# A decoder layer's feed-forward block on one NeuronCore: gate and up projections as seven half-size block products

## The reference

```python
def _ffn(x, w_gate, w_up, w_down, g, b):
    hdn = jax.nn.silu(x @ w_gate) * (x @ w_up)
    return _layer_norm(ALPHA * x + hdn @ w_down, g, b)
```

## Time and profile before

| what | value |
|---|---|
| median of three runs | 1817.17 us (1814.51 to 1818.33) |
| profiled execution, its span | 1820.0 us |
| TensorE busy | 1761.5 us (97%), 11328 matmuls |
| VectorE busy | 703.3 us (39%) |
| ScalarE busy | 371.5 us (20%) |
| GpSimd busy | 513.6 us (28%) |
| TensorE's mean granted clock | 0.975 of full speed |
| chain of work that ended last | TensorE 85%, VectorE 7% |

### The profile page before, as it was taken

One profiled execution on the slowest core, in us unless ns is written; L12 is line 12 of the kernel. 1 busy time (PEld: TensorE's weight loads), 2 busy tenths in 40 slices (PEclk: granted clock), 3 DMA queues, 4 the chain that ended last, 5 costly groups with the idle time before them and its releaser, 6 DMA issues.

```text
span 1820.0 us, 29093 instructions
## 1 busy us (share of the span) xinstructions
PE 1761.5 (97%) x11328; PEld 1615.3 (89%) x11328; DVE 703.3 (39%) x1255; ACT 371.5 (20%) x699; POOL 513.6 (28%) x296
## 2 busy tenths in 40 slices
PE   7999999998999999999999999999999999999995
PEld 6967677776877879999999899999999999999994
DVE  4156767541335261111174833313312312322327
ACT  4133232322233231111120640010010010010033
POOL 4210111110212023333353823333333333333325
PEclk9899999998998889999999999999999999999998
DMA  5144434304641122111112211111111111111102
GB/s 158 59 112 131 124 116 145 117 12 128 191 135 27 47 50 56 47 46 46 47 47 58 82 47 47 47 46 46 46 46 46 46 46 47 51 45 48 50 25 93
DMA packets 175297, 127.54 MB, mean 70 GB/s; under 512 B 22362, under 2 KB 148730, under 8 KB 175218
## 3 DMA queue, kind: packets, MB, share of 16 engines
q1 hardware_dynamic: 169586, 125.12, 23.3%
q10 hardware_dynamic: 5632, 1.35, 0.5%
HBM read 116.57 MB, written 9.87 MB: 69 GB/s over the span
## 4 chain that ended last, share of the span: by engine, by line
PE 85%; DVE 7%; DMA 2%; ACT 2%; issue 2%; SPq 2%; POOL 0%; DVEq 0%; ACTq 0%; POOLq 0%
PE psum L794 13%; PE psum L798 13%; PE psum L797 13%; PE psum L1355 4%; PE psum L1354 4%; PE psum L1350 4%; PE psum L855 4%; PE psum L859 4%; PE psum L861 4%; PE psum L1010 3%; PE psum L1303 2%; PE psum L1307 2%; PE psum L1306 2%; PE psum L983 2%; PE psum L939 1%
## 5 line engine op out<-in xcount | busy, mean ns | idle before, releaser
L733 POOL CAST wh<-raw 128x1024 fp32r<-128x1024 f32 x131 | 145.8, 1113 | 1258.9 <-PE psum L855 389.4
L794 PE MATMUL psum<-xh,wh 128*128 128x344 f32 (+1 forms) x1392 | 449.0, 323 | 3.6 <-POOL wl L735 3.4
L797 PE MATMUL psum<-xl,wh 128*128 128x344 f32 (+1 forms) x1392 | 446.2, 321 | 0.0
L798 PE MATMUL psum<-xh,wl 128*128 128x344 f32 (+1 forms) x1392 | 446.2, 321 | 0.0
L735 POOL TENSOR_TENSOR wl<-raw,wh 128x1024 fp32r<-128x1024 f32 x131 | 333.3, 2545 | 10.5
L794 PEld LDWEIGHTS psum<-xh,wh 128*128 128x128 f32 x1392 | 263.5, 189 | 5.3 <-issue 5.3
L797 PEld LDWEIGHTS psum<-xl,wh 128*128 128x128 f32 x1392 | 263.5, 189 | 0.5 <-issue 0.5
L798 PEld LDWEIGHTS psum<-xh,wl 128*128 128x128 f32 x1392 | 263.3, 189 | 0.0
L2457 DVE TENSOR_TENSOR hf<-sg,psum 128x344 f32<-128x344 f32 x66 | 33.8, 513 | 372.8 <-PE psum L798 363.7
L855 PE MATMUL psum<-xh,wh 128*128 128x352 f32 (+1 forms) x480 | 162.8, 339 | 1.5 <-DVE ql L1992 1.5
L859 PE MATMUL psum<-xl,wh 128*128 128x352 f32 (+1 forms) x480 | 161.1, 336 | 0.0
(11 more groups left out here) (332 smaller groups left out, 2702.7 us busy)
## 6 DMA issues: line engine op xcount, KB each, us to landing
raw<-in_w_in SPq DMA_DIRECT2D x86, 256.0 KB, 3.3
parts<-in_cache_k SPq DMA_DIRECT2D x64, 256.0 KB, 3.0
parts<-in_cache_v SPq DMA_DIRECT2D x64, 256.0 KB, 2.9
raw<-in_w_gate SPq DMA_DIRECT2D x44, 256.0 KB, 3.1
raw<-in_w_up SPq DMA_DIRECT2D x44, 256.0 KB, 3.1
raw<-in_w_down SPq DMA_DIRECT2D x44, 256.0 KB, 2.7
raw<-in_w_o SPq DMA_DIRECT2D x28, 256.0 KB, 3.1
cb<-negc_scratch SPq DMA_DIRECT2D x8, 520.0 KB, 5.4
```

What stands on the lines that cost most here:

```text
L733: pool.tensor_copy(wh[:, s, :], raw[:, r, :]).then_inc(sem("panel_high"), 1)
L794: first = mm(out, w[0], x[0], start=(n == 0), stop=False)
L797: mm(out, w[0], x[1], start=False, stop=False)
L798: last = mm(out, w[1], x[0], start=False, stop=(n == len(ks) - 1))
```

## The change

For groups 1 to 10 the product of a weight block by the activations, 256 by 1024 by 1032 for gate and again for up, is cut in two along each of the three sizes. The plain product of 2 x 2 blocks takes eight block products; the change makes it from seven with sums of blocks (Winograd's form of Strassen's method). With half sizes: hidden 128, model width 512 (four blocks of 128), tokens 516 (TH), which TensorE takes as two chunks of 258 columns (CW). One product is 2 x 4 x 3 = 24 matmuls.

- **Weights.** SP loads quarters of 128 by 512, 256 KB each (`quarter`), into six halves of `raw`. GpSimd makes the sums S1 = c + d, S3 = a - c, S2 = S1 - a, S4 = b - S2, and splits seven units of 512 columns for gate, seven for up and four for down, 18 a group, into six places of `wh` and `wl`; a place is free when TensorE has ended the unit six before (`room`, by `unit_done`).
- **Activations.** Three differences of blocks of x1 and a fourth that replaces a quarter of `xh` and `xl` are made once, in group 0, by VectorE (`t_make`, `t_low`) and ScalarE (`t_high`).
- **Products and combinations.** TensorE makes A11, S1, S3, S2, each in its own pair of banks, then A12, A22 and S4, which add onto the banks of A11, S3 and S1. ScalarE copies A11 and S1 out before that (`snaps`). VectorE makes the other blocks from these by adds (`combine`, and one add of two SBUF blocks, `c22`), ScalarE applies SiLU to gate's four blocks, and for up VectorE multiplies and splits the four hidden blocks.
- **Down** has its three chunks of 344 as before, from the new places (`down_new`); at its first chunk it waits for three of the four hidden blocks, and in its last chunk it tells GpSimd twice that weights are free, by waiting for its own last matmul.
- **Group 10** turns `mixed` within up's last three products, and makes the nine y tiles one after the other behind them.
- The loops over groups 1 to 9 on all engines are written out. Some buffers move.

The diff, cut to its core:

```diff
+UNITS_A_GROUP = 18
+A11, S1, S3, S2, A12, A22, S4 = range(7)
+BANKS_OF = {A11: 0, A12: 0, S1: 2, S4: 2, S3: 4, A22: 4, S2: 6}
+DOWN_BANKS = [6, 7, 0, 1, 4, 5, 2, 3]
...
+            def room(g):
+                if g >= 6:
+                    pool.wait_ge(sem("unit_done"), g - 5)
+                else:
+                    pool.wait_ge(sem("panel_used"), PAN_FFN + 4 + g // 2)
+            def unit_from(g, source):
+                high, lower = unit_of(wh, g), unit_of(wl, g)
+                step(pool.tensor_copy(high, source))
+                pool.tensor_tensor(lower, source, f(high), ALU.subtract).then_inc(sem("panel_split"), 1)
...
+                    come(n, ha, 0)
+                    room(g + A11)
+                    unit_from(g + A11, a)
+                    come(n, hc, 0)
+                    come(n, hd, job_)
+                    room(g + S1)
+                    s1 = unit_of(wlf, g + S1)
+                    step(pool.tensor_tensor(s1, c_, d, ALU.add))
+                    step(pool.tensor_tensor(c_, a, c_, ALU.subtract))
+                    step(pool.tensor_tensor(a, s1, a, ALU.subtract))
+                    unit_from(g + S1, s1)
...
-            with pe.Fori(0, FGROUPS - 2) as g:
-                B.loop(g, FFN_PER)
-                p = PAN_FFN + 6 + 6 * g
-                job(p, 0, A3, ALL8, X8, chunks=BODY)
-                job(p + 1, 1, B3, ALL8, X8, chunks=BODY)
-                job(p + 2, 2, A3, ALL8, X8, chunks=BODY)
-                job(p + 3, 0, B3, ALL8, X8, chunks=BODY)
-                down(g + 1, p)
-                B.end(FGROUPS - 2)
...
+            def product(n, job_, v, after=None):
+                g = unit_no(n, job_, v)
+                pe.wait_ge(sem("panel_split"), PANELS + g + 1)
+                b, begins = BANKS_OF[v], v in (A11, S1, S3, S2)
+                for c in range(2):
+                    out = psum[:, b + c, 0:CW]
+                    for k in range(4):
+                        x = moving(v, k, c)
+                        cols = slice(k * P, k * P + P)
+                        first = mm(out, wH[:, cols], x[0], start=(begins and k == 0), stop=False,
+                                   skip_group_check=True)
...
+                        mm(out, wH[:, cols], x[1], start=False, stop=False, skip_group_check=True)
+                        last = mm(out, wL[:, cols], x[0], start=False, stop=(k == 3), skip_group_check=True)
+                    if c == 0 and after is not None:
+                        after()
+                last.then_inc(sem("unit_done"), 1)
...
+            def seven(n, job_, turns=None):
+                for v in (A11, S1, S3, S2):
...
+                    product(n, job_, v)
+                pe.wait_ge(sem("snapped"), 2 * j + 1)
+                product(n, job_, A12, turns)
...
+                pe.wait_ge(sem("combined"), 4 * j + 2)
+                product(n, job_, A22, turns)
+                pe.wait_ge(sem("snapped"), 2 * j + 2)
+                product(n, job_, S4, turns)
+            def down_new(n):
+                for c, (c0, cw) in enumerate(BODY):
+                    pe.wait_ge(sem("hidden_split"), 6 + 4 * (n - 1) + (3 if c == 0 else 4))
+                    for m in range(KT):
...
+                            if c == 2 and m % 4 == 3 and k == 0:
+                                last.then_inc(sem("unit_done"), 1)
+                        give(b, last)
+                        if c == 2 and m % 4 == 3:
+                            pe.wait_ge(bank_full[b], B.before(b))
+                            pe.sem_inc(sem("unit_done"), 1)
...
+            for n in range(1, FGROUPS - 1):
+                seven(n, 0)
+                seven(n, up)
+                down_new(n)
...
+            seven(FGROUPS - 1, 0)
+            seven(FGROUPS - 1, up, turn_y)
+            pe.wait_ge(sem("panel_split"), PANELS + UNITS_A_GROUP * (FGROUPS - 1))
+            turn_y()
             y_tile(0)
+            turn_y()
             y_tile(1)
-            unit(0, UP_LAST[1], 1, (xh, xl))
-            unit(2, GATE_LAST[2], 2, (xh, xl))
+            turn_y()
+            for i in range(2, NT):
                 y_tile(i)
...
+            skip(A3)
+            for c in range(3):
+                hidden(0, c)
+            for n in range(3):
+                t_make(n)
+            t_low(0)
+            t_low(1)
+            skip(A3)
+            for c in range(3):
+                hidden(1, c)
+            t_make(3)
...
+                product_done(n, job_, A22)
+                combine(n, job_, 2, c21, c12, 4)
+                if job_:
...
+                    hid(block(1, 0), c21)
+                    hid_low(n, 1)
+                    hid_low(n, 2)
+                product_done(n, job_, S4)
+                combine(n, job_, 3, c12, c12, 2)
+                if job_:
...
+                    hid(block(0, 1), c12)
+                    hid_low(n, 3)
```

More of the change, by code:

```diff
@@ new lines, in _ @@
+            for n in range(1, FGROUPS):
+                for job_ in range(2):
+                    g = unit_no(n, job_, 0)
+                    ha, hb, hc, hd = (x[job_] for x in (HALF_A, HALF_B, HALF_C, HALF_D))
+                    a, b, c_, d = (half_of(raw, h) for h in (ha, hb, hc, hd))
+                    come(n, ha, 0)
[9 more added lines that the diff above has]
+                    unit_from(g + S1, s1)
+                    room(g + S3)
+                    unit_from(g + S3, c_)
+                    room(g + S2)
+                    unit_from(g + S2, a)
+                    come(n, hb, job_)
+                    room(g + A12)
+                    unit_from(g + A12, b)
+                    room(g + A22)
+                    unit_from(g + A22, d)
+                    room(g + S4)
+                    s4 = unit_of(wlf, g + S4)
+                    step(pool.tensor_tensor(s4, b, a, ALU.subtract))
+                    unit_from(g + S4, s4)
+                for q, h in enumerate(HALF_DOWN):
+                    come(n, h, 1)
+                    room(unit_no(n, 2, q))
+                    unit_from(unit_no(n, 2, q), half_of(raw, h))
@@ new lines, in hid_high @@
+            def hid_high(n, x):
+                u, h = ((1, 1), (0, 0), (1, 0), (0, 1))[x]
+                act.wait_ge(sem("hidden"), 6 + 4 * (n - 1) + x + 1)
+                do(hh[:, u, TH * h:TH * h + TH], block(u, h), ACT.Copy).then_inc(sem("hidden_high"), 1)
+            for n in range(1, FGROUPS - 1):
+                snaps(n, 0)
+                gate_silus(n)
+                snaps(n, 1)
+                for x in range(4):
+                    hid_high(n, x)
+            snaps(FGROUPS - 1, 0)
@@ L2475, in _, with product_done @@
                                                     op0=ALU.mult, op1=ALU.add))
+                if c < 2:
+                    t_low(2 + c)
             for b in range(8):
                 settled(b)
[L2478 to L2483 removed]
+            def product_done(n, job_, v):
+                dve.wait_ge(sem("unit_done"), unit_no(n, job_, v) + 1)
@@ new lines, in hid, with hid_low @@
+            def hid(g_, u_):
+                ve.tensor_tensor(g_, g_, u_, ALU.mult).then_inc(sem("hidden"), 1)
+            def hid_low(n, x):
+                u, h = ((1, 1), (0, 0), (1, 0), (0, 1))[x]
+                cols = slice(TH * h, TH * h + TH)
+                dve.wait_ge(sem("hidden_high"), 6 + 4 * (n - 1) + x + 1)
+                ve.tensor_tensor(hl[:, u, cols], sg[:, u, cols], f(hh[:, u, cols]), ALU.subtract)\
+                    .then_inc(sem("hidden_split"), 1)
+            for n in range(1, FGROUPS):
+                combinations(n, 0)
+                combinations(n, 1)
+                if n == FGROUPS - 1:
+                    break
@@ L2491, in _ @@
                     settled(b)
-                B.end(FGROUPS - 2)
-            skip(A3)
-            for c in range(3):
-                hidden(FGROUPS - 1, 0, c)
             def moments(i):
```

435 lines of the change are left out of this document (290 added, 145 removed).

## The result

The changed kernel takes 1825.53 us (median of four runs, 1824.81 to 1829.88), beside 1817.04 for the kernel before on the same chip: 1.0053 times as long, with an interval of 1.0035 to 1.0071. It is slower by half a per cent, where 1807 was forecast as the likeliest time.

A forecast was written before the change was run, and what follows sets the result against it. TensorE alone was taken to set the pace. Groups 1 to 9: 9 x (-4.8 + 0.8 + 1.6) = -21.6; group 0 +10.3, group 10 +1.1: -10.2 from 1817.2 gives 1807 us, range 1787 to 1838.

The forecast's parts named there:

- Part 1: Gate and up matmuls: 336 of 258 columns, 119.5 ns apart, replace 288 of 344, saving 4.8 us a group.
- Rival 4: Gate and up: narrow matmuls don't get cheaper in proportion, so the saving is gone: 1855 us; chance 0.04.
- straight-line estimate: Gate and up matmuls: by the skill's figures 98 ns each, a loss of 1.5 us a group.
- Part 2: Down's last chunk: TensorE's two waits for its own last matmul cost 0.8 us a group (0.5 to 0.9).
- Part 3: Start of down: TensorE stalls for hidden blocks, 1.6 us a group, between 0.4 and 2.9 depending on GpSimd's turns.
- rival 1: Start of down: GpSimd stays out of the way, stall 0.4 us, groups 1 to 9 gain 32.4: 1787; chance 0.18.
- rivals 2 and 3: Start of down: two lost turns, stall 2.9 us; with full clock 1819 (0.16), with falling clock 1835 (0.23).
- rival 3: Start of down: two lost turns, and 2.9 us idle lets TensorE's clock fall, 3.5 us each: 1835 to 1850; chance 0.23.
- Part 4: Other waits within groups: all covered, with GpSimd's 41 us of work fitting the group's 65.
- Rival 5: Products: GpSimd can't keep up with 18 units, TensorE waits for weights, some 3 us a group: 1834; chance 0.03.
- Part 5: Group 0: down starts 6.3 us later and a half clock adds 4, together +10.3 us (+0.7 to +11).
- Part 6: Last group and tail: nine y tiles one after the other, first at 51 us; group lasts 99.0, +1.1 us.

The follow-up runs named there:

- hold_a11: Changed kernel, but in groups 2 to 10 GpSimd waits before splitting A11 until three hidden blocks of the group before are split: 1797.58 us.
- dummy_matmuls: Changed kernel plus 16 unused matmuls of 258 columns on TensorE before its wait ahead of each down of groups 1 to 9: 1814.06 us.
- gain_early: Changed kernel, but the last layer norm's gain and bias are loaded into weight-buffer slots once down's first two units of group 10 are split: 1822.09 us.
- low_earlier: Changed kernel, but VectorE makes the low part of hidden block (0,0) before waiting for up's product A22: 1825.85 us.
- group0_lows: Changed kernel, but group 0's low parts of the x1 differences move behind the hidden blocks and between down's chunks: 1821.22 us.
- no_drains: Changed kernel, but in down's last chunk the next matmul signals free weights, without TensorE waiting for its own last matmul: 1807.31 us.
- hold_s1: Changed kernel, but GpSimd waits for the three hidden blocks only before the S1 sum, after splitting A11: 1805.30 us.
- four_edits: Changed kernel with hold_a11, gain_early, no_drains and all four of group 0's low parts moved between and behind down's chunks: 1779.67 us.
- one_gpsimd_shift: four_edits, but in the tail GpSimd adds the layer norm's shift for the first tile only, VectorE for the rest: 1778.36 us.

## Why the prediction was wrong, step by step

- **Part 1 held.** After's matmuls of 258 columns start 0.12 us apart:

```profile
1247.05 0.28 PE L1532 MATMUL psum<-xl,wh 128*128 128x258 f32 x1
1247.17 0.28 PE L1533 MATMUL psum<-xh,wl 128*128 128x258 f32 x1
1247.29 0.28 PE L1528 MATMUL psum<-xh,wh 128*128 128x258 f32 x1
```

  The 336 of them that fill 40.52 us come 120.6 ns apart, against 119.5 taken. Without gaps a group takes 63.36 (571.1/9 is 63.46, with one wait of 1.0 left in group 1), 4.47 less than 67.83; forecast were 4.8. Rival 4 falls. So does the straight-line estimate that the prediction drew from the Trainium skill, "TensorE: Matmul & The Clock Gate", section "Back-to-back issue gap": it would have had 98 ns here.
- **Part 2 held.** Drains: 0.87 a group, forecast 0.8, bounds 0.5 to 0.9. What the step left out is the clock: with the drains gone it fell four times less often, another 6 us, by a way that isn't shown.
- **Part 3 was mis-sized, within its ends.** The stall is 2.04, forecast 1.6 between 0.4 and 2.9. The mechanism was the right one, and rival 1, GpSimd out of the way, had its size: its nine groups were to gain 32.4, and hold_a11 gains 32.0 against the kernel before (610.4 to 578.4). That the two agree so well is partly luck: the wait is nothing there and not 0.4, and the matmuls gain 4.47 and not 4.8. What failed is the middle that I took between the ends. The requests lie so near to each other that I thought turns would fall either way; in fact they fell alike in all nine groups, and a turn was lost to both GpSimd steps each time. By turns it is the case of rivals 2 and 3, but two turns cost 2.04 and not 2.9 (2.8 by the terms of the prediction itself).
- **The step that turned the sign is the clock.** The forecast had full clock in groups 1 to 9; rival 3, with 0.23, had it fall. It did, in six of nine, behind 2.04 us of waiting. With the wait filled and the clock up, dummy_matmuls is no longer slower than the kernel before (0.9987). A fall costs 1.5 us, not 3.5: the 3.5 came from half of the 7 us of the earlier trace rows, and here the clock is at half for 3.4. My argument against, that 65 us of dense work might excuse a gap, is refuted for six groups.
- **Groups 1 to 9 in one line.** Per group -4.47 + 0.87 + 2.04 + 6 x 1.5/9 = -0.56; measured (605.41 - 610.44)/9 = -0.56. Forecast: -2.4. This is 16.6 us of the error: 9.0 from the clock, 4.0 from the stall, 3.6 from matmuls and drains.
- **Part 4 held.** GpSimd is busy for 46.1 us of a group's 66.3 (forecast 41, with turns lost up to 47), and among TensorE's waits from group 0's end on none is for weights. Rival 5 falls.
- **Part 5 was a little too dear.** Down of group 0 started 5.3 later (forecast 6.3) and ran at half clock for 5.3 us, which cost 2.5 (forecast 4).
- **Part 6 missed a load.** The first y tile came at 51, as forecast, but the layer norm's gain is loaded behind the ninth y copy. Before, that lay under the work between the tiles; now the copies end 8.6 us after the first tile was begun (1774.75, 1766.11), and the load needs another 6. I had counted SP's loads of weights and not this one. It cost 3.2, and a lost turn at VectorE's first shift 2.1, the price the prediction named without putting it in. The other 0.7 lies in smaller differences: even without the load the gain begins at 59.9 (gain_early), where 58.8 was forecast.
- **Sum.** With 16.6 and 6.0 added and 2.4 taken off, the forecast of 1807 becomes 1827, beside 1825.5 measured; the traced stages differ by 9.9, the medians by 8.5. The changed kernel's time lies in the range, above the likeliest case's own.

## What to carry to other kernels

A change that takes work off the bounding engine puts the other engines' chains at its seams, and one seam in each of nine groups can eat the gain. Cost each seam with the steps of both engines that take turns there, and if who comes first hangs on a tenth of a microsecond, don't take the middle: make the engine that isn't urgent wait, which here was one wait and 28 us. Then ask of each gap what it does to TensorE's clock, and of each load in the shortened stretch what had hidden it.

## What the runs showed of the hardware that I had not expected

**Gaps and the clock.** Nine downs in each kernel:

| kernel | TensorE's wait ahead of down | two drains a group | downs with the clock at half |
|---|---|---|---|
| changed kernel, low_earlier, group0_lows, gain_early | 2.04 | yes | 6 in each |
| no_drains | 2.04 | no | 2 |
| hold_s1 | 0.97 | yes | 0 |
| dummy_matmuls | 2.04, all but 0.16 filled with matmuls | yes | 0 |
| hold_a11 | none | yes | 0 |
| four_edits, one_gpsimd_shift | none but 1.0 and 0.9 in group 1 | no | 0 |

Behind a wait of 2.04 us the clock falls 0.2 to 1.5 us after work has begun again, and is back 3.4 us later, in each of the 26 falls; behind group 0's 5.18 it had fallen 1.4 us before the wait ended. The wait alone doesn't decide: with the same 2.04 everywhere, groups 1, 3 and 7 keep full clock in the changed kernel and in group0_lows, and groups 1, 4 and 8 in low_earlier and gain_early. Taking away the two drains, which show no fall of their own, took the falls from six to two; by what way isn't shown.

**Turns are exact.** VectorE and GpSimd took turns at the same place in every group, so that the wait was 2.04 or 2.05 in all 45 downs of five kernels; 0.16 us in who comes first cost the multiply 1.1 us in low_earlier, and the wait stayed at 2.04, with one low part less in the seam. The Trainium skill, "SBUF — State Buffer", section "Who interferes with whom", says that a VectorE step with two SBUF inputs contends with GpSimd's reads, and that the order of issue decides which of the two blocks the other. The rows agree: the multiply of 0.69 took 1.77 behind a subtraction that had begun 0.09 earlier. GpSimd's casts are held up too: one of 0.61 took 0.85 in hold_a11 (at 1212.19) and 1.00 in low_earlier (at 1217.92), beside a multiply and a low part of VectorE.
